# A triangular inverse from 32x32 diagonal blocks instead of 64x64, inside a fused hybrid layer

## What is computed

```python
n_mat = jnp.where(strict, -jnp.einsum('nbhid,nbhjd->nbhij', kb, kc) * decay, 0.0)
t_mat = jnp.eye(CHUNK, dtype=f32) + n_mat
p_mat = n_mat
for _ in range(int(math.log2(CHUNK)) - 1):
    p_mat = jnp.einsum('nbhij,nbhjk->nbhik', p_mat, p_mat)
    t_mat = t_mat + jnp.einsum('nbhij,nbhjk->nbhik', t_mat, p_mat)
```

## Time and profile before

| | |
|---|---|
| three runs | 2707.76, 2709.22, 2709.70 us; median 2709.22 |
| profiled execution | 2707.76 us; its span from the first to the last instruction is 2706.0 us |
| TensorE | matmuls 2682.5 us (99%), 19808 records; weight loads 2274.0 us |
| VectorE, ScalarE, GpSimd | 1416.5 us (52%), 971.0 us (36%), 398.7 us (15%) |
| granted TensorE clock | 0.999 of full speed over the span |

### The profile page before, as it was taken

One profiled execution on the slowest core, in us unless ns is written; L12 is line 12 of the kernel. 1 busy time (PEld: TensorE's weight loads), 2 busy tenths in 40 slices (PEclk: granted clock), 3 DMA queues, 4 the chain that ended last, 5 costly groups with the idle time before them and its releaser, 6 DMA issues.

```text
span 2706.0 us, 50329 instructions
## 1 busy us (share of the span) xinstructions
PE 2682.5 (99%) x19808; PEld 2274.0 (84%) x19808; DVE 1416.5 (52%) x3633; ACT 971.0 (36%) x3158; POOL 398.7 (15%) x238
## 2 busy tenths in 40 slices
PE   7999999999999999999999999999999999999998
PEld 6888888888888888888888888888888888888887
DVE  6777777233366666612236666651224666665012
ACT  4555455422244444421124444442112444444101
POOL 4333333443100110000000110000000011000000
PEclk9999999999999999999999999999999999999999
DMA  7554554787733333255453333335546333333564
GB/s 249 201 180 167 182 193 170 264 288 279 253 121 111 128 128 117 107 203 217 172 219 130 112 114 125 130 110 203 216 172 220 113 118 128 123 112 125 183 222 171
DMA packets 79001, 458.43 MB, mean 169 GB/s; under 512 B 13232, under 2 KB 17456, under 8 KB 31792
## 3 DMA queue, kind: packets, MB, share of 16 engines
q1 hardware_dynamic: 65664, 427.85, 44.2%
q10 hardware_dynamic: 13104, 27.36, 3.0%
HBM read 352.42 MB, written 102.76 MB: 168 GB/s over the span
## 4 chain that ended last, share of the span: by engine, by line
PE 96%; DMA 2%; POOL 1%; DVE 1%; ACT 0%; issue 0%; POOLq 0%; SPq 0%; ACTq 0%; DVEq 0%
PE bank L1305 24%; PE bank L1307 23%; PE bank L1306 23%; PE bank L1450 2%; PE last_banks L1450 2%; PE last_banks L1415 2%; PE bank L1434 2%; PE last_banks L1434 2%; PE bank L1403 2%; PE bank L1499 1%; PE bank L1491 1%; PE bank L1475 1%; PE last_banks L1557 1%; PE bank L1483 1%; PE bank L1548 1%; PE bank L1538 1%
## 5 line engine op out<-in xcount | busy, mean ns | idle before, releaser
L1305 PE MATMUL bank<-hT_hi,w_sl 128*128 128x512 f32 x2112 | 872.8, 413 | 0.0
L1307 PE MATMUL bank<-hT_hi,w_sl 128*128 128x512 f32 x2112 | 827.3, 392 | 0.0
L1306 PE MATMUL bank<-hT_lo,w_sl 128*128 128x512 f32 x2112 | 825.5, 391 | 0.0
L1307 PEld LDWEIGHTS bank<-hT_hi,w_sl 128*128 128x128 f32 x2112 | 396.7, 188 | 86.1
L1305 PEld LDWEIGHTS bank<-hT_hi,w_sl 128*128 128x128 f32 x2112 | 398.3, 189 | 71.6 <-issue 0.7
L1306 PEld LDWEIGHTS bank<-hT_lo,w_sl 128*128 128x128 f32 x2112 | 398.8, 189 | 65.4 <-issue 0.7
L436 POOL TENSOR_TENSOR w_sl<-w_raw,w_sl 128x1024 fp32r<-128x1024 f32 x90 | 218.3, 2430 | 391.2 <-ACT w_sl L517 381.6
L982 DVE SCALAR_TENSOR_TENSOR area<-zraw,stc,area 128x512 f32<-128x512 f32 x288 | 220.2, 765 | 4.2
L1148 DVE SCALAR_TENSOR_TENSOR s_cur<-s_cur,scs,last_banks 128x128 f32<-128x128 f32 x112 | 38.9, 348 | 199.8 <-PE last_banks L1554 199.8
L611 ACT ACTIVATE area<-area 128x512 f32<-128x512 f32 x96 | 60.4, 629 | 219.6 <-DVE area L982 219.6
L455 POOL TENSOR_TENSOR gu<-mk,g_hi 128x512 fp32r<-128x512 f32 x32 | 41.9, 1309 | 643.7 <-DVE nmx L1102 603.8
(11 more groups left out here) (244 smaller groups left out, 4817.7 us busy)
## 6 DMA issues: line engine op xcount, KB each, us to landing
w_sl<-saved_w SPq DMA_DIRECT2D x270, 1024.0 KB, 4.8
saved_w<-w_sl SPq DMA_DIRECT2D x90, 1024.0 KB, 4.9
w_raw<-in_w_tiles SPq DMA_DIRECT2D x90, 512.0 KB, 5.9
area<-in_x ACTq DMA_DIRECT2D x4, 2048.0 KB, 10.4
area<-in_x ACTq DMA_DIRECT2D x14, 512.0 KB, 8.1
out_y<-area ACTq DMA_DIRECT2D x3, 2048.0 KB, 8.1
bias_sb<-in_bias ACTq DMA_DIRECT2D x32, 128.0 KB, 2.3
out_y<-area SPq DMA_DIRECT2D x4, 512.0 KB, 2.7
```

Of the source, the lines that this page charges most:

```text
L1305: pe.matmul(dst, a_hi, b_hi, start=first, stop=False)
L1306: pe.matmul(dst, a_hi, b_lo, start=False, stop=False)
L1307: return pe.matmul(dst, a_lo, b_hi, start=False, stop=last)
```

## The change

The doubling works on the four 32x32 diagonal blocks of each tile, on four diagonal places of the array, with LEVELS = 4. What lies between two 32x32 blocks of one 64x64 block is put in by a new step, two small products `inner_in` and `inner_out`, with a copy on ScalarE and two on VectorE. VectorE makes the transposed blocks: for the first powers (instead of ScalarE's copy of TensorE's transpose) and for the new step. The sum of the identity's four blocks, `stacked`, is made once. TensorE's `fill(2)` ahead of `merge_in` becomes `fill(1)` three times. The semaphores of the merge are renamed into three counters. The diff, cut to what matters:

```diff
-LEVELS = 5
-LAST = 2 ** LEVELS
+BL = 32
+LEVELS = 4
...
+def merges(n1, step):
+    return (n1 - 1) * 3 + step
...
+        BLOCKS = tuple(slice(r, r + BL) for r in range(0, P, BL))
+        CORNERS = ((BLOCKS[0], BLOCKS[1]), (BLOCKS[2], BLOCKS[3]))
+        yt, vt = p_sb[1][:, :, 0:BL], p_sb[1][:, :, BL:2 * BL]
...
ScalarE:
-                    act.activation(p_sb[l % 2][:, PAIR[g], 0:width], pv(bank[P_BANK[g]])[:, PAIR[g], 0:width], ACT.Copy).then_inc(p_ready[g], 1)
+                    act.activation(p_sb[l % 2][:, PAIR[g], 0:BL], pv(bank[P_BANK[g]])[:, PAIR[g], 0:BL], ACT.Copy).then_inc(p_ready[g], 1)
...
-                for lo, hi in HALVES:
-                    ins = act.activation(ptt[lo:hi, :, 0:CH], tt[lo:hi, :, lo:hi], ACT.Copy)
+                for r in BLOCKS:
+                    ins = act.activation(ptt[r, :, 0:BL], tt[r, :, r], ACT.Copy)
...
-                for lo, hi in HALVES:
-                    act.activation(p_sb[0][lo:hi], bch(5)[lo:hi, :, lo:hi], ACT.Copy)
...
+                act.wait_ge(merge_product, merges(n1, 1))
+                act.activation(yt, bch(5)[:, :, 0:BL], ACT.Copy).then_inc(merge_act, 1)
...
VectorE:
+            dve.tensor_reduce(stacked[:, :], mk[:, IDENT, :].rearrange("p (a c) -> p c a", c=BL), AX, ALU.add).then_inc(dve_init, 1)
...
-                for lo, hi in HALVES:
-                    ins = dve.tensor_tensor(ptt[lo:hi, :, CH:P], tt[lo:hi, :, lo:hi],
-                                            mk[lo:hi, IDENT:IDENT + 1, lo:hi].to_broadcast([CH, NT, CH]), ALU.add)
-                ins.then_inc(tt0_ready, 1)
...
+                def first_powers():
+                    dve.wait_ge(pt0_ready, n1)
+                    dve.wait_ge(ssq_ready[0], n1)
+                    dve.transpose(p_sb[0][:, :, 0:BL], ptt[:, :, 0:BL]).then_inc(p0_ready, 1)
+                    dve.tensor_tensor(ptt[:, :, BL:2 * BL], ptt[:, :, 0:BL],
+                                      stacked[:, None, :].to_broadcast([P, NT, BL]), ALU.add).then_inc(tt0_ready, 1)
...
-                        copy(ptt[:, PAIR[g], 0:CH], a[:, PAIR[g], 0:CH]).then_inc(pt_ready[g], 1)
+                        copy(ptt[:, PAIR[g], 0:BL], a[:, PAIR[g], 0:BL]).then_inc(pt_ready[g], 1)
...
-                def settled():
...
+                def diagonal():
                     for g in range(2):
                         dve.wait_ge(tt_ready[g], n1 * (LEVELS - 1))
+                        dve.wait_ge(a_done[g], n6 + (LEVELS + 1))
+                    for i in (0, 2, 1, 3):
+                        r = BLOCKS[i]
+                        ins = dve.tensor_tensor(tt[r, :, r], bch(A_BANK[0])[r, :, BL:2 * BL], ptt[r, :, BL:2 * BL], ALU.add)
+                        if i in (0, 2):
+                            ch.inc(ins)
+                    ins.then_inc(diag_ready, 1)
                     ch.sync()
+                    for a, _ in CORNERS:
+                        ins = dve.transpose(vt[a], tt[a, :, a])
+                    ins.then_inc(merge_dve, 1)
+
+                def inner_corners():
+                    dve.wait_ge(merge_product, merges(n1, 2))
+                    for a, c in CORNERS:
+                        ins = copy(tt[a, :, c], bch(7)[a, :, 0:BL])
+                    ins.then_inc(merge_dve, 1)
...
                 logits(0)
+                first_powers()
                 attention()
...
TensorE, square and apply:
-                        for lo, hi in HALVES:
-                            ins = pe.matmul(pv(bank[P_BANK[g]])[lo:hi, t, 0:width], ptt[lo:hi, t, 0:CH], p_sb[(l - 1) % 2][lo:hi, t, 0:width], start=True, stop=True)
+                        for r in BLOCKS:
+                            ins = pe.matmul(pv(bank[P_BANK[g]])[r, t, 0:BL], ptt[r, t, 0:BL], p_sb[(l - 1) % 2][r, t, 0:BL], start=True, stop=True)
...
-                    c0, c1 = (0 if l < LEVELS else first_column(l)), (P if l > 1 else CH)
+                    c0, c1 = (0 if l < LEVELS else BL), (2 * BL if l > 1 else BL)
+                    dst = bch(A_BANK[g if l <= LEVELS else 0])
...
+                        for r in BLOCKS:
+                            ins = pe.matmul(dst[r, t, c0:c1], p_sb[(l - 1) % 2][r, t, 0:BL], ptt[r, t, c0:c1], start=True, stop=True)
...
+                def inner_in():
+                    pe.wait_ge(merge_dve, merges(n1, 1))
+                    for t in range(NT):
+                        for a, c in CORNERS:
+                            ins = pe.matmul(bch(5)[c, t, 0:BL], tt[a, t, c], vt[a, t, :], start=True, stop=True)
+                    ins.then_inc(merge_product, 1)
+
+                def inner_out():
+                    pe.wait_ge(merge_act, merges(n1, 2))
+                    pe.wait_ge(diag_ready, n1)
+                    for t in range(NT):
+                        for a, c in CORNERS:
+                            ins = pe.matmul(bch(7)[a, t, 0:BL], yt[c, t, :], tt[c, t, c], start=True, stop=True)
+                    ins.then_inc(merge_product, 1)
...
                 apply(LEVELS + 1, 0)
                 apply(LEVELS + 1, 1)
-                fill(2)
+                fill(1)
+                inner_in()
+                fill(1)
+                inner_out()
+                fill(1)
                 merge_in()
```

## The result

The changed kernel took 2833.88 us (median of 4 runs, 2829.89 to 2839.66) where the kernel before took 2709.19 on the same chip: ratio 1.0463, 95% interval [1.0444, 1.0481], 4.6% slower. The prediction said 2694, range 2676 to 2727, and slower with a chance of 0.25. It said faster with a chance of 0.6, so it was wrong in sign, and the time lies outside its range. The span grew by 125.9 us, from 2706.0 to 2831.9.

A forecast was written before the change was run, and what follows sets the result against it. TensorE, matmuls busy 99% of the span, was taken as the bound. Per head 0.22 - 0.71 = -0.49 us, x 32 = -15.7; 2707.76 - 15.7 + 0.3 = 2692.4, plus 1.5 for the median, about 2694; range 2676 to 2727.

The forecast's parts named there:

- The matmuls: Squares and applies in the levels: 0.126 us for a 32-column stage on four places, 0.232 us for a 64-column apply.
- The common limit of the places: Rival: records no closer than 14.5 ns on any places, so each 32-column stage costs 0.232 us; 2727 us, chance 0.15.
- the floor: Rival: 29 ns between record starts everywhere, a stage 0.46 us, merge_in about 5 us later a head; 2865 us, chance 0.03.
- Changes of the tiling: TensorE switching between 64x64 and 32x32 places: 0.14 us each, so each of the two quarters costs 0.28 more.
- The loop of a level: From apply through VectorE's copy and the square back to apply: 0.94 us or more, against 0.72 of TensorE work a level.
- The transposes: VectorE's two 32-partition transposes ahead of inner_in: 0.27 and 0.29 us, like any 128-element operation.
- The new wait: TensorE idles 1.09 us a head before inner_in, waiting for VectorE's adds and transposes.
- The levels end at 4.87 instead of 7.54, a gain of 2.67 us: Time from the first square to the end of the last applies in a head, about 0.5 us of it TensorE idle.
- The full clock: Wide matmuls behind the levels were priced at 0.23 or 0.24 us; no cost was put on a clock fall.
- rival C: Follow-up rival: TensorE loses its clock because of the small matmuls and all the rest follows; no chance given.
- Costed at nothing: First powers' transpose and stacked add on VectorE, its conversions and the head's end: no cost; uncovered, 10 us over 32 heads.
- way to merge_in: From the first square to merge_in in a head: 9.45 us instead of 9.23, with one more fill step, worth 0.71, behind it.

The follow-up runs named there:

- e13: Changed kernel with two more fill steps behind level 3, taken from the head's end, eleven kept ahead of the levels: 2758.9 us, ratio 1.0187.
- e7: Changed kernel with one VectorE add over 128 partitions and one transpose ahead of inner_in, instead of four adds and two transposes: 2781.56 us, ratio 1.0264.
- e19: Changed kernel, nine fill steps ahead, two behind level 3, weight load held, one add and transpose before inner_in, diagonal blocks by PSUM adds: 2703.31 us, ratio 0.9985.
- the paused one: Kernel before with two useless VectorE reductions ahead of the copy of level 4, so TensorE pauses once a head: 2755.15 us, ratio 1.0171.
- the two doubled ones: Kernel before with squares and applies of levels 2 and up repeated on idle 64x64 places: 2763.4 us; the same with the weight load held: 2760.37 us.
- e4: Kernel before with squares and applies of levels 2 and up issued again on the two idle 64x64 places, results unread: 2763.4 us, ratio 1.0197.
- e5: Changed kernel with two of the eleven fill steps ahead of the levels moved behind level 3: 2776.07 us, ratio 1.0249.

## Why the prediction was wrong

*The matmuls* (0.126 and 0.232 us a stage): right, if a little low. Squares stand 0.15 from the next stage and 64-column applies 0.23. The common limit of the places did not show, nor did the floor: 16 records start between 2543.30 and 2543.45, 9 ns apart. The Trainium skill ("TensorE: Matmul & The Clock Gate", section "Wait — 56ns, not 53.3ns?") says that matmuls never start less than about 25 ns apart. Across places these records do; on any one place they are 31 to 53 ns apart, which fits it.

*Changes of the tiling* (0.14): right. The quarters start 0.71 us after the first square and the next level at 1.29; the sum had 0.69 and 1.27.

*The loop of a level* (0.94): right; level 3 starts 2.28 us after the first square, predicted 2.22.

*The transposes*: right. Two take 0.62 us, 301 ns each over the span, predicted 0.29. The four adds take 1.15 where 1.08 was summed. The new wait, 1.09 predicted, is 1.23 where the clock holds.

```profile
L1077 DVE TENSOR_TENSOR area<-last_banks,area 32x128 f32<-32x128 f32 x128 | 36.7, 287 | 39.2 <-PE last_banks L1460 36.7
...
L1083 DVE STREAM_TRANSPOSE area<-area 32x128 f32<-32x128 f32 x64 | 19.3, 301 | 1.4
```

*"The levels end at 4.87 instead of 7.54, a gain of 2.67 us"*: this is the step that failed. Its array time is about right (5.03), but it took for granted that TensorE has its instructions when the array is free. It works off 256 records in 2.0 us where it had 4.8, and in 32 of 32 heads the next ones were not there: 1.3 to 2.6 us each time and once more 0.3, 59.4 in all. No rival had it. The trace of before offered the data: 160 instruction packets for 39616 matmuls and weight loads and the waits between them, 256 of them worked off in 4.8 us, and two short stops, one of them listed on "issue".

*The full clock.* This is the other step that failed. The sum priced every wide matmul behind the levels at 0.23 or 0.24 us, and the 1.09 us of new idle time at 1.09. It put no cost on a fall of the clock, and 210 us ran at half clock. Over all the runs listed, 640 heads, I took the idle time of TensorE between the first square and merge_in and looked whether the granted clock fell there or within 5 us behind:

```
idle time in the head    heads    with a fall of the clock
under 1.0 us              191        0
1.0 to 1.5                132       27
1.5 to 2.0                129       75
over 2.0                  188      143
```

After's heads have both the stop and the wait, and the clock fell in 30 of 32. With the wait nearly alone (e13) it fell in 7, with the stops alone (e7) in 18. Taking out the wait (e7) took 93 us of half clock away with the stops nearly unchanged, and in e19 the same 32x32 stages run at a clock of 0.999. Of the 191 heads without a fall in the first row, 133 are of kernels with 32x32 places. So rival C falls: the small matmuls by themselves did not lower the clock, and it fell less as idle time was taken out. The 64x64 kernels lost their clock less often at the same idle time (7 of 59 heads between 1.0 and 1.5 us, and 1 of 9 between 1.5 and 2.0, for the kernel before, the paused one and the two doubled ones; 20 of 73 and 74 of 120 for the 32x32 ones), so the kind of work around the idle time may count too; that was not separated.

*Costed at nothing*: the first powers' transpose, the converted weights and the head's end cost nothing that these runs could see, but 4.4 us in which TensorE's transposes of N wait for VectorE, in the 8 heads of block 0.

*How much is shown.* That the stops come with record density and shrink when time is put between the levels is shown by e4, e5, e13 and e19; they did not go in any version. That they are the arrival of 256-record packets rests on their remainder and on the 555 of 570 that end 1.1 to 1.7 us after a packet; nothing here changed the packets themselves. How the 82 us divide between half clock and small terms (0.25 us a head, 8 us, between the predicted and the measured way to merge_in) is a remainder, not a measurement.

## What to carry to other kernels

Before cutting work into smaller instructions, count how many TensorE reads per microsecond: here 256 records in 2.0 us stopped it in every head, in 3.3 to 3.6 us by anything from nothing to 1.0 us (e19), and what helped was to put long matmuls between the short ones and to keep a weight load from their way. An idle stretch of a microsecond can cost more than a microsecond when another lies near it: in after, with two of them in a head, the clock of what follows was halved in 30 of 32 heads, and what is left over for it (82 us) is about as much as the idle stretches themselves. And a copy on VectorE from SBUF to SBUF on the path should be looked at where GpSimd works; here an add with an operand in PSUM was not held up.

## What the runs showed of the hardware

- After an instruction packet of 256 TensorE records has ended, 1.1 to 1.7 us pass until TensorE goes on (555 of 570 stops in 20 traces). In after that is 3.3 to 4.6 us after the record 256 back; the packet between starts 0.9 to 2.1 us after that record and takes 0.9 to 1.4 us.
- Records on four 32x32 places start 9 ns apart on average, at 0.15 us a stage of 16, and 31 to 53 ns apart on one place.
- The clock fell in none of 191 heads with less than 1.0 us of idle time in this part, and in 143 of 188 with more than 2.0.
- VectorE: four copies of 32x128 from SBUF to SBUF took 3.01 us beside a GpSimd operation of 2.35 us, against 0.87 without it; four adds with an operand in PSUM took 1.15 with or without one.
